# Sixteen gather buffers and two weight slots instead of twelve and three, in a routed two-block transformer kernel

## The reference, cut to what matters

```python
def peer_ffn(x, w_q, sub_keys, u, v):
    q = (xt @ w_q).reshape(T, PEER_HEADS, 2, PEER_HALF)
    s = jnp.einsum('thcd,hcnd->thcn', q, sub_keys)
    ...  # top 16 of each half, then top 16 of the 256 sums: 8 heads x 16 picks
    def expert_block(args):           # blocks of 128 tokens
        ub = jnp.take(u, eb, axis=0)
        act = gelu(einsum('thkd,td->thk', ub, xb))
        vb = jnp.take(v, eb, axis=0)
        return einsum('thk,thkd->td', gb * act, vb)
```

## Time and profile before

| | us |
|---|---|
| median of 3 runs | 2260.46 |
| lowest, highest | 2255.74, 2270.28 |
| span of the profiled execution | 2259.6 |

### The profile page before, as it was taken

How to read it: one execution, slowest core, us unless ns; L and a number is a source line. 1 busy time by engine, 2 the same in 40 slices (tenths; PEclk the granted TensorE clock), 3 DMA queues, 4 the chain that set the end, 5 groups by cost and what they waited for, 6 DMA issues and landing times. The chain is left out here.

```text
span 2259.6 us, 17114 instructions
## 1 busy us (share of the span) xinstructions
PE 1527.2 (68%) x5282; PEld 879.4 (39%) x5282; DVE 1450.5 (64%) x3168; ACT 323.1 (14%) x778; POOL 985.0 (44%) x1058
## 2 busy tenths in 40 slices
PE   8987600467656539776573897666576656899998
PEld 7446600222225225422341552235252232376453
DVE  1236898779587875678688468786978676444101
ACT  1220100011112111111120111111321000123111
POOL 0102466667665555566455456653446444000000
PEclk9989855688867669987766899778767877899999
DMA  7436999999999999999999999999989999973672
GB/s 260 85 117 245 394 408 409 337 360 370 371 379 403 404 406 358 361 365 367 407 399 405 365 342 368 375 401 386 391 293 403 399 398 399 366 243 130 242 260 93
DMA packets 268005, 760.62 MB, mean 337 GB/s; under 512 B 21295, under 2 KB 46590, under 8 KB 267275
## 3 DMA queue, kind: packets, MB, share of 16 engines
q0 software_dynamic: 147456, 536.94, 61.8%
q1 hardware_dynamic: 120458, 222.60, 27.8%
HBM read 756.84 MB, written 2.62 MB: 336 GB/s over the span
## 5 line engine op out<-in xcount | busy, mean ns | idle before, releaser
L946 POOL DMA_INDIRECT ROWS<-in_peer_u,IDX x512 | 483.3, 944 | 455.5 <-DVE ROWS L991 266.9
L946 POOL DMA_INDIRECT ROWS<-in_peer_v,IDX x512 | 487.8, 953 | 357.2 <-PE bank L292 121.4
L991 DVE SCALAR_TENSOR_TENSOR ROWS<-ROWS,XP 128x1024 f32<-128x1024 f32 x512 | 602.3, 1215 | 23.7 <-issue 12.3
L995 DVE SCALAR_TENSOR_TENSOR XP<-ROWS,GATE,XP 128x1024 f32<-128x1024 f32 x316 | 405.8, 1284 | 155.9 <-DMA ROWS<-in_peer_v,IDX 133.7
L292 PE MATMUL bank<-ROWS,DG 128*128 128x512 f32 x774 | 380.0, 649 | 94.2 <-DMA ROWS<-in_peer_v,IDX 78.5
L292 PE MATMUL bank<-ring,XT 128*128 128x512 f32 (+6 forms) x912 | 392.7, 589 | 62.3 <-DMA ring<-in_ffn_w_up 32.0
L292 PEld LDWEIGHTS bank<-ring,XT 128*128 128x128 f32 x912 | 185.6, 214 | 249.9 <-issue 179.4
L292 PEld LDWEIGHTS bank<-ROWS,DG 128*128 128x128 f32 x774 | 157.5, 209 | 309.8 <-issue 201.8
L292 PE MATMUL bank<-XT,ring 128*128 128x128 f32 (+2 forms) x1504 | 209.4, 301 | 57.1 <-issue 27.4
L292 PEld LDWEIGHTS bank<-XT,ring 128*128 128x128 f32 (+1 forms) x1504 | 198.3, 204 | 71.8 <-issue 35.7
L307 PE MATMUL bank<-CN,X 128*128 128x128 f32 x128 | 27.1, 384 | 184.9 <-issue 90.7
(11 more groups left out here) (408 smaller groups left out, 1461.6 us busy)
## 6 DMA issues: line engine op xcount, KB each, us to landing
ring<-in_peer_w_q SPq DMA_DIRECT2D x16, 2048.0 KB
ring<-in_ple_w_gate SPq DMA_DIRECT2D x9, 2048.0 KB
ring<-in_ffn_w_gate SPq DMA_DIRECT2D x8, 2048.0 KB
ring<-in_ffn_w_up SPq DMA_DIRECT2D x7, 2048.0 KB
ring<-in_a_w_in SPq DMA_DIRECT2D x6, 2048.0 KB
ring<-in_w_in SPq DMA_DIRECT2D x6, 2048.0 KB
ring<-in_ffn_w_down SPq DMA_DIRECT2D x6, 2048.0 KB
ROWS<-in_peer_u,IDX POOLq DMA_INDIRECT x512
```

Of the source, the lines that this page charges most:

```text
L946: G.indirect_dma_start(ROWBUF[slot(n, c)][:, :], None, tables[table], bass.IndirectOffsetOnAxis(IDX[:, tt, c:c + 1], axis=0)).then_inc(row ...
L991: V.scalar_tensor_tensor(row, row, 1.0, XP[:, :], ALU.mult, ALU.mult, accum_out=ACTV[:, tt, c:c + 1]).then_inc(row_used, 1)
L995: V.scalar_tensor_tensor(XP[:, :], row, gate, XP[:, :], ALU.mult, ALU.add).then_inc(row_used, 1)
```

## The change

- 16 row buffers in passes 0 to 5, 12 from pass 6 on (`NARROW = 6`). The slots of a pass are counted from pass 6 anew, and the row that last held a buffer is looked up (`last_user`).
- Two ring slots in passes 0 to 5. From pass 6 on the last four rows (`LATE`) are the third slot; its first load waits until pass 5 is used up. Total memory is the same.
- The first 14 blocks go to slots that are written out (`FIRST_SLOT`): the two ring slots and, while there are no rows yet, the four pieces of the row buffer (slot 3 is rows 0 to 3, slot 4 is rows 4 to 7, slot 5 is rows 8 to 11, slot 2 is rows 12 to 15).
- The four query blocks of layer 0 are loaded once (four loads of 2 MB fewer). Tile 1 reads the kept ones in the order 2, 3, 0, 1. Blocks 2 and 3 lie in rows 8 to 15.
- So pass 0 gets new waits on POOL: before row 0 for the projection's blocks in rows 0 to 7 to be read (`out_w_read`), before row 8 for tile 1's queries 2, before row 12 for tile 1's queries 3 (`kept_read`).

```diff
-SLOTS = 12
+SLOTS = 16
-RING, SLOT = 3, 4096
+RING, SLOT = 2, 4096
+LATE = SLOTS * D // SLOT - 1
+NARROW = 6
+KEPT_SLOT = {2: 5, 3: 2}
+FIRST_SLOT = {"a_gate": 0, "a_q": 1, "a_k": 3, "a_v0": 4, "a_v1": 0, "a_og0": 1, "a_og1": 3, "keys0": 0, "a_out0": 4, "a_out1": 3,
+              "peer_q0_0": 1, "peer_q0_1": 0, "peer_q0_2": KEPT_SLOT[2], "peer_q0_3": KEPT_SLOT[3]}
...
-        ring += [ROWS[:, i * SLOT // D:(i + 1) * SLOT // D, :].rearrange("p s d -> p (s d)") for i in range(MORE)]
+        ring += [ROWS[:, i * SLOT // D:(i + 1) * SLOT // D, :].rearrange("p s d -> p (s d)") for i in (LATE, *range(LATE))]
...
-            slot_no.append(n % RING if not last_gather else (n - last_gather[0] + RING) % (RING + MORE))
-            slot_use.append(slot_no[:n].count(slot_no[n]))
+            if key in FIRST_SLOT:
+                slot = FIRST_SLOT[key]
+            elif not fewer_rows:
+                slot = (n - len(FIRST_SLOT)) % RING
+            elif not last_gather:
+                slot = (n - fewer_rows[0]) % (RING + 1)
+            else:
+                slot = (n - last_gather[0] + RING + 1) % (RING + MORE)
+            slot_no.append(slot)
+            slot_use.append(slot_no[:n].count(slot))
...
         enter_route(0, "0")
-        enter_cols("peer_q01_", a["peer_w_q"][0], [0, 512, 1024, 1536, 2048])
...
+        fewer_rows.append(len(stream))
         enter_ple(1, "10")
...
-                    if n == RING:
+                    if n == 3:
...
-                    if before:
-                        sp.wait_ge(*released[before[-1]])
-                    elif n >= RING:
+                    if n == fewer_rows[0] + RING:
+                        sp.wait_ge(row_used, dve_used(NARROW - 1))
+                        sp.wait_ge(pe_used, tensor_used(NARROW - 1))
+                    elif last_gather[0] <= n < last_gather[0] + MORE - 1:
                         sp.wait_ge(row_used, dve_used(len(passes) - 1))
                         sp.wait_ge(pe_used, tensor_used(len(passes) - 1))
+                    elif before:
+                        sp.wait_ge(*released[before[-1]])
+                    elif n == place["peer_q0_3"]:
+                        sp.wait_ge(S("phase_end"), 3)
...
         def slot(n, c):
-            return (n * PICKS + c) % SLOTS
+            if n < NARROW:
+                return (n * PICKS + c) % SLOTS
+            return ((n - NARROW) * PICKS + c) % (SLOTS - SLOT // D)
+
+        row_users = [[(n, c) for n in range(len(passes)) for c in range(PICKS) if slot(n, c) == s] for s in range(SLOTS)]
+        turn_of = {pick: i for users in row_users for i, pick in enumerate(users)}
...
+        def last_user(n, c):
+
+            i = turn_of[n, c]
+            return row_users[slot(n, c)][i - 1] if i else (-1, 0)
...
-                m, h = divmod(n * PICKS + c - SLOTS, PICKS)
+                m, h = last_user(n, c)
...
+                if n == 0 and c in (8, 12):
+                    G.wait_ge(S("kept_read"), c // 4 - 1)
...
+                    if n == 0:
+                        pool.wait_ge(S("out_w_read"), 1)
...
-                        weight_read(f"peer_q{tag}_{e}", f"q{e}{tiles[0]}")
+                        if l == 1:
+                            weight_read(f"peer_q{tag}_{e}", f"q{e}{tiles[0]}")
...
-                    for e in range(4):
-                        pe.wait_ge(*landed(f"peer_q{l}{tt}_{e}"))
-                        queries(slot_of(f"peer_q{l}{tt}_{e}"), tt, e)
-                        weight_read(f"peer_q{l}{tt}_{e}", f"q{e}{tt}")
+                    for e in (2, 3, 0, 1):
+                        queries(slot_of(f"peer_q{tag}_{e}"), tt, e)
+                        weight_read(f"peer_q{tag}_{e}", f"q{e}{tt}")
...
                     if l == 0 and e == 2:
+                        A.sem_inc(S("out_w_read"), 1)
                         act_norm_root(1)
...
-                    for e in range(4):
+                    for e in (2, 3, 0, 1):
                         act_queries(tt, e)
+                        if e in KEPT_SLOT:
+                            A.sem_inc(S("kept_read"), 1)
```

More of the change, by code:

```diff
@@ L190, in build @@
         slot_no, slot_use = [], []
-        last_gather = []
+        fewer_rows, last_gather = [], []
         def enter(key, ap):
@@ L920, in slot @@
         def slot(n, c):
-            return (n * PICKS + c) % SLOTS
+            if n < NARROW:
[3 more added lines that the diff above has]
+        turn_of = {pick: i for users in row_users for i, pick in enumerate(users)}
         def arrived(n, c):
-            return row_in[slot(n, c)], 16 * ((n * PICKS + c) // SLOTS + 1)
+            return row_in[slot(n, c)], 16 * (turn_of[n, c] + 1)
+        def last_user(n, c):
+            i = turn_of[n, c]
+            return row_users[slot(n, c)][i - 1] if i else (-1, 0)
         def dve_used(n, k=None):
```

## The result

The changed kernel takes 2304.97 us, the median of 4 runs (2300.20 to 2319.03), beside 2258.10 of the kernel before in the same measurement: a ratio of 1.021, with a 95% interval of 1.017 to 1.025. It is 47 us slower where 45 us less were forecast. Its profiled execution has a span of 2298.5 us against 2259.6, so 38.9 us of the loss can be looked for in the two traces.

What follows compares the result with a forecast made beforehand. It took row-buffer depth to bound passes 1, 3 and 5, and a PE, ACT, DVE chain passes 2 and 4. From 2259.6 us, −16 −15 −13 −13 +5 +5 +2 = −45 gave 2215 us, range 2182 to 2252.

Steps and rivals of the forecast that it cites:

- Pass 0: Four loads of 2.1 MB fall away, against 10 us of idle engines from the hold: −16 us, bounds 4 to 22 gained.
- DVE must follow: Pass 0: DVE starts scores 3 9 us earlier and uses rows at 1.22 us, under 1.29, so keeps up with fetches.
- the hold of pass 0 eats the saved loads: Rival: pass 0 gains only 0 to 4 us and the other gains come, about 2229 us; chance 0.12.
- Passes 1, 3 and 5: Four more row buffers shrink POOL's stalls: −15, −13 and −13 us, bounds 5 to 22 gained for each pass.
- the buffer's depth bounds these passes: Passes 1, 3, 5: DVE and PE starve in turn, neither full; four more buffers shrink a stall by up to 5.0 us.
- consumers set the pace: Rival, shared passes: PE's own rhythm delays POOL, four rows gained once per pass, 2241 us; chance 0.20 together with memory ceiling.
- The sign that I had named: The forecast is wrong if the shared passes (1, 3, 5) keep 1.42 us a row.
- rival of a memory ceiling: Shared passes: 361 to 364 GB/s is what single-row reads get; about 2241 us, chance 0.20 together with "consumers set the pace".
- Passes 2 and 4: Ring of two: some loads in embed and attention come later, +5 us a tile, bounds 0 and 16.7.
- This one is covered by what delayed PE there; that cause I can't name: Embed, passes 2 and 4: the second gate block, ready for ACT at 658.5 us against 665.83 before, costs nothing.
- ring of two uncovers the chain: Rival, passes 2 and 4: no load there hides, 48 us a tile, 2297 us; slower case, chance 0.07.
- Pass 6: The second gate block of tile 0's last embed loads after pass 5: +2 us, bounds 0 and 5.

Runs made afterwards that it cites:

- e3: The changed kernel with its two ring slots swapped from the second layer's keys on; 2285.58 us, ratio 1.014 to the kernel before.
- e5: The changed kernel with 12 rows and three ring slots again, the ring walked the other way round from the keys on; 2264.42 us, ratio 1.001.
- f2: e2's kernel once more, on a chip of the second kind beside f1; by the medians f1 is 11 us faster.
- f3: e5's kernel once more, on the same second-kind chip as f1 and f2; ratio 0.999 to the kernel before.
- f1: The changed kernel once more, on a chip of the second kind; ratio 1.0021 to the kernel before.
- e2: The changed kernel with 12 row buffers in all passes, the ring still of two until pass 6; 2295.33 us, ratio 1.020.
- e4: The changed kernel, but row 8 of pass 0 waits for all four query blocks of tile 1; 2296.24 us, ratio 1.020.
- e9: e5's kernel with PE taking five rows instead of six between two query blocks in passes 3 and 5; second kind, 2199.74 us, ratio 1.003.

## Why the prediction was wrong

**Before 208 us.** Forecast 0, measured −2.1. Right.

**Pass 0, −16 forecast, +15.7 measured** (by DVE's rows it is 19.5 us late at the end of the pass). The hold went nearly as worked out: row 8 at 232.34 us and row 12 at 239.49, forecast 227 and 234. The step that failed is the sentence "DVE must follow". I followed the two query blocks that the hold needs and stopped. Blocks 0 and 1 and the keys' transposes come behind them on PE, and DVE uses rows again only after those, at 290.58. The keys' load, which I didn't cost, went from 248.34 to 277.67, for it now waits for the last block in the order, in the same slot. e3 prices that at 9 us, e5 at 12 with three slots (by DVE's rows 7 and 17). The rest is PE's slow stretch, which no row of mine bounded; my bounds of 4 to 22 left out a loss. The trace of the kernel before had a shorter one, which I didn't show and didn't count: tile 0's block 3 runs from 213.23 to 228.30, 15 us, with such pauses, where I took 7.2 a block. This is the place of the rival "the hold of pass 0 eats the saved loads", for which I had said "a chain of PE, ACT and DVE steps must all come early". On the second kind, where PE ran through with the DMA engines full, pass 0 was 185.4, not far from the 182 that the forecast implies. That is no hit: what the kernel before takes there isn't known, and f2 and f3, with 12 rows, are as fast by DVE's rows (189.1 and 191.6, f1 189.1).

**Passes 1, 3 and 5, −41 forecast, −5.6 measured.** The step that failed is "the buffer's depth bounds these passes". From "both sides starve in turn" it doesn't follow that a deeper line helps: e2 has the same times with 12. The waits for rows did shrink, and that gave no time: a wait of one consumer is not on the path only because it is long. On the first kind PE and DVE are held up for some us at a time without a cause in the trace. I read the passes so, that this time isn't made up whatever the buffers hold; that is argued from equal times with 12 and 16, not shown by a run that takes the pauses away alone. Four buffers then give four rows once and are full ever after, as the rival "consumers set the pace" said; but even its 3 × 5 us weren't there. On the second kind pass 1 reached the 409 GB/s that I had counted on, 168.2 us against a forecast of 174, but so it does with 12 (f2: 166.9). I had charged to the depth what was a hold-up of the engines. Only in passes 3 and 5 of the second kind did depth give something: 3 us in pass 3 and, by my estimate above, some 5 of the 10 in pass 5, where the forecast had 13 each. The sign that I had named, 1.42 us a row kept in the shared passes, came on the first kind: 104 rows in 153 us are 1.47. Nor is the range of rates that I read in the earlier trace rows, 340 to 409 GB/s, right: slice 30 has 293. The rival of a memory ceiling falls by 409 GB/s with shared rows. That is also above the share of about 358 GB/s that the Trainium skill ("HBM Reference", section "Specifications (TRN2)") gives for a core whose neighbour streams too, and the neighbour was idle here.

**Passes 2 and 4, +10 forecast, +23.1 measured.** The mechanism was right, its size was not. "This one is covered by what delayed PE there; that cause I can't name" (so the prediction) was the weak sentence: without knowing what covered the second gate block I took it as covered. It was not: 15.6 us of wait in f1, near the 16.7 that I had kept as a bound, and 26.2 in the changed kernel's pass 4. With the query projection (7.4) and the down projection (4.3) PE waits 27.3 us a tile for the ring in f1, and in the changed kernel's pass 4 at least 34.1 (26.2 and 7.9), past the 28 that I had named as a sign of being wrong. The pass is longer by only 7 to 15, since with three slots PE waits longer for the other engines: in f3 30.3 us for DVE at L320 and 21.8 for ACT, in f1 14.9 and 12.4. That is the rival "ring of two uncovers the chain". Its place was right, but its rule that a wait costs its full length was not. Its sum was wrong too: 96 us against the 57 of gain, with the 2 of pass 6 added to the loss, is +41 or 2301, not 2297. That the span measured, 2298.5, lies near both is luck: of the 84 us between the forecast and the span, 72 are in the gains that didn't come.

**Pass 6, +2 forecast, +7.7 measured by POOL's cuts, −1.7 by DVE's.** The 7.7 us are POOL's longer lead, which is given up when the buffers go from 16 to 12, and no loss. The third slot's first block is issued late, as forecast (1485.69 us, when pass 5's rows are used), but PE reads it at 1515.91 without a wait. The blocks behind it come no later in the pass than before: 46 us after POOL's first fetch of it, against 57. On the second kind pass 6 is 8 to 10 us longer by DVE's rows (f1 against f3 and f2). There the 2.1 MB that the pass has more are 5 us at 409 GB/s; the rest stays open. e3, in which the last query block and the next gate block no longer share a slot, gains nothing here (253.1 against 251.0 by DVE's rows).

**The sum.** By DVE's cuts, terms of −57 for depth and saved loads measured +15 (19.5 up to the end of pass 0, −4.4 in passes 1, 3 and 5), and terms of +12 for the ring +24. The rivals leaned on the same thought: each was worked out as less of a gain, and only one as a loss.

## What to carry to other kernels

More buffers help only where the waits for them lengthen the pass: follow one stall, and if with more buffers it merely moves by that many rows, depth isn't the bound. Where a step is moved ahead, follow the queue to the last instruction that the next engine waits for, and ask of every load which slot it takes and who frees that slot last. A cover that can't be named isn't one: keep the uncovered load as the expected value. And cut a span at the engine that does the work, not at the one that runs ahead: a deeper buffer moves the latter's marks without saving any time.

## What the runs showed of the hardware

- PE can run slowly while row fetches fill the DMA engines. On the first kind of chip a query block took 31 us instead of 7.3, with 22 matmuls in 24 us, at 399 GB/s; with the fetches held back (e4) it took 7.3. On the second kind it took 7.2 with the DMA engines full (f1), and on the first kind other blocks did so too (kernel before, 233.73 to 265.30 us). What slows PE is not named in the trace. That it is the supply of instructions is my guess.
- The same program takes 2194 us on some chips and 2253 to 2263 on others, 3%, with the same durations of single instructions (in pass 1 of e9 and of e5: PE's row matmuls 642 and 660 ns, rows on DVE 1281 and 1281). Pass 1 is 167 to 171 us on the faster and 185 to 190 on the slower ones, with 12 rows or 16. The mean granted clock of the kernel before is 0.807 to 0.818 on the faster and 0.801 to 0.811 on the slower. What differs in the chips stays open, and with it whether the idle time without a name is a pause or data that land late unrecorded.
- A change can be 2% slower on the one kind and the same on the other. A ratio measured on one chip is a ratio for its kind.
